# A transformer block with a mixture of experts: when the hidden rows are turned, and which engine loads the slot records of extra tokens

## The reference

```
x <- x + W_out [ gnorm(stick-breaking attention(h)) ++ gnorm(sliding-window GQA(h)) ] + b_out,  h = RMSNorm(x)
logits = RMSNorm(x) @ w_router + b_router          # 32 experts
top 4 of 32 per token, softmax over the four = gates
per chosen expert e, per token row:
    gu  = row @ w_gate_up[e] + b_gate_up[e]         # 1024 -> 2048
    act = (clip(up, -7, 7) + 1) * g * sigmoid(1.702 g),   g = min(gate, 7)
    y   = act @ w_down[e] + b_down[e]               # 1024 -> 1024
x <- x + sum of gate * y over the four;  output RMSNorm_final(x)
```

## Time and profile before

| | |
|---|---|
| median of 3 runs | 2253.32 us (2247.72 to 2255.8) |
| profiled execution | 2252.55 us, span 2250.4 us |
| granted TensorE clock, mean | 0.95 |
| busy: TensorE / VectorE / ScalarE / POOL | 94% / 68% / 65% / 14% |
| chain that ended last | TensorE 71%, VectorE 12%, issue 9%, ScalarE 4% |
| expert loop | item 0 starts at 768.49 us, the last item ends at about 2209 us |

### The profile page before, as it was taken

One profiled execution on the slowest core, in us unless ns is written; L12 is line 12 of the kernel. 1 busy time (PEld: TensorE's weight loads), 2 busy tenths in 40 slices (PEclk: granted clock), 3 DMA queues, 4 the chain that ended last, 5 costly groups with the idle time before them and its releaser, 6 DMA issues.

```text
span 2250.4 us, 37586 instructions
## 1 busy us (share of the span) xinstructions
PE 2108.3 (94%) x11367; PEld 1606.5 (71%) x11368; DVE 1521.1 (68%) x1908; ACT 1468.0 (65%) x1944; POOL 323.4 (14%) x327
## 2 busy tenths in 40 slices
PE   5999999999988499999999999999999999999997
PEld 4777777777766377878777777777776777676683
DVE  4355455553545678888888777787786688675585
ACT  4456565653332378888788687787785687675583
POOL 1000000001123211202011121111111121010022
PEclk9899999958989599999999999999999999999996
DMA  6300000110113789999899898899897899797694
GB/s 193 60 24 19 19 20 19 50 73 29 58 39 116 266 268 381 370 381 372 292 342 334 289 342 291 298 377 296 290 376 244 282 338 318 279 313 242 221 318 176
DMA packets 250409, 507.19 MB, mean 225 GB/s; under 512 B 44454, under 2 KB 62676, under 8 KB 250228
## 3 DMA queue, kind: packets, MB, share of 16 engines
q1 hardware_dynamic: 234724, 462.98, 58.4%
q0 software_dynamic: 15632, 43.53, 7.5%
HBM read 470.25 MB, written 38.54 MB: 226 GB/s over the span
## 4 chain that ended last, share of the span: by engine, by line
PE 71%; DVE 12%; issue 9%; ACT 4%; DMA 2%; POOL 1%; SPq 0%; DVEq 0%; ACTq 0%; POOLq 0%
PE bank L1001 23%; PE bank L1023 12%; PE bank L773 8%; PE bank L1035 6%; DVE w_low L1799 6%; PE bank L871 4%; PE bank L1052 3%; PE bank L826 2%; PE bank L853 2%; PE bank L801 2%; PE bank L816 2%; PE bank L842 2%; PE bank L1117 1%; PE bank L991 1%; DVE act_low L1813 1%
## 5 line engine op out<-in xcount | busy, mean ns | idle before, releaser
L1799 DVE TENSOR_TENSOR w_low<-gu_w,w_high 128x1024 fp32r<-128x1024 f32 x528 | 620.0, 1223 | 242.2 <-ACT w_high L1357 234.0
L1357 ACT CAST w_high<-gu_w 128x1024 fp32r<-128x1024 f32 x528 | 534.9, 1050 | 163.4 <-PE bank L1001 86.7
L1001 PE MATMUL bank<-w_high,x_high 128*128 128x512 f32 x1056 | 416.1, 394 | 3.0 <-DVE w_low L1799 3.0
L1001 PE MATMUL bank<-w_high,x_low 128*128 128x512 f32 x1056 | 413.9, 392 | 0.0
L1001 PE MATMUL bank<-w_low,x_high 128*128 128x512 f32 x1056 | 413.3, 391 | 0.0
L1799 DVE TENSOR_TENSOR w_low<-dn_w,w_high 128x1024 fp32r<-128x1024 f32 x264 | 315.1, 1225 | 19.5 <-ACT w_high L1357 13.2
L1357 ACT CAST w_high<-dn_w 128x1024 fp32r<-128x1024 f32 x264 | 270.8, 1050 | 23.1 <-PE bank L1001 13.4
L1023 PE MATMUL bank<-w_high,act_high 128*128 128x512 f32 x528 | 212.6, 403 | 23.9 <-DVE act_low L1813 23.9
L1001 PEld LDWEIGHTS bank<-w_high,x_high 128*128 128x128 f32 x1056 | 199.0, 188 | 46.6 <-DVE w_low L1799 3.8
L1001 PEld LDWEIGHTS bank<-w_high,x_low 128*128 128x128 f32 x1056 | 198.8, 188 | 42.8
L1001 PEld LDWEIGHTS bank<-w_low,x_high 128*128 128x128 f32 x1056 | 199.1, 189 | 42.1
(11 more groups left out here) (223 smaller groups left out, 3136.7 us busy)
## 6 DMA issues: line engine op xcount, KB each, us to landing
gu_w<-in_w_gate_up SPq DMA_DIRECT2D x528, 512.0 KB, 11.3
dn_w<-in_w_down SPq DMA_DIRECT2D x132, 1024.0 KB, 18.4
w_st<-in_w_in SPq DMA_DIRECT2D x14, 512.0 KB, 4.8
xt<-in_x SPq DMA_DIRECT2D x8, 512.0 KB, 4.4
wo_sb<-in_w_out SPq DMA_DIRECT2D x2, 2048.0 KB, 9.7
x<-in_x SPq DMA_DIRECT2D x8, 512.0 KB, 4.2
residual_rows<-x SPq DMA_DIRECT2D x8, 512.0 KB, 2.7
h_rows<-h SPq DMA_DIRECT2D x8, 512.0 KB, 2.9
```

The costliest lines, as they stand in the source:

```text
L1001: mm = pe.matmul(bank[:, 2 * h + g, :], a[:, k, :], b, start=False, stop=last)
L1357: act.copy(w_high[:, u % RING, :], src).then_inc(high_ready, 1)
L1799: dve.tensor_tensor(w_low[:, u % RING, :], raw, w_high[:, u % RING, :], ALU.subtract).then_inc(split_ready, 1)
```

## The change

On TensorE the second half is turned after three down units instead of four. On ScalarE `silu` follows `room` directly in both halves, with the casts that stood between them behind; the cast of unit 23 goes behind `act_high`. VectorE's order follows: the product of each half stands directly behind the clamp, unit 23's split behind `act_low`.

The six loads of the extra rows' records leave SP's `load_slots`. ScalarE issues them (`over_slots`), in the branch of `extra_rows` in which the next item has extra tokens, ahead of the wait for `xo_psum`. They count on a semaphore of their own, `d_over_slot`, which the other branch raises by the same 96. For their addresses ScalarE loads the next item's expert and first slot into registers in every pass, waits for the item's own `d_over_slot` and steps `act_passed`. POOL's `scatter` and ScalarE's `gated_rows` wait for `d_over_slot` too.

```diff
-SLOT_LOADS = 16 * (2 + sum(PARTS))
+SLOT_LOADS, OVER_LOADS = 16 * 2, 16 * sum(PARTS)
...
                 words(0, 0, P, 0, 0)
                 words(0, 1, EXTRA, P, 0)
-                word = 2
-                for k, parts in enumerate(PARTS):
-                    m = P // parts
-                    for q in range(parts):
-                        words(m * q, 2 + k, m, P, word)
-                        word += 2
...
             def scatter(n, step):
                 n_tok = tokens_of(n)
                 pool.wait_ge(slots_ready, n + 1)
+                pool.wait_ge(d_over_slot, OVER_LOADS * n + OVER_LOADS)
...
-                down(i, range(4))
+                down(i, range(3))
                 turn_hidden(i, 1)
+                down(i, range(3, 4))
                 by_class(n_tok, lambda parts: turn_over(i, parts))
...
+            def over_slots(n, e, first):
+                word = 2
+                for k, parts in enumerate(PARTS):
+                    m = P // parts
+                    for q in range(parts):
+                        act.dma_start(slot_in[m * q:m * q + m, bass.ds(8 * n + (12 + 2 * k), 2)],
+                                      slots[e, bass.ds(first + P, m), word:word + 2]).then_inc(d_over_slot, 16)
+                        word += 2
+
-            def extra_rows(n, n_tok):
+            def extra_rows(n, n_tok, e, first):
                 with act.If(n_tok > P):
+                    over_slots(n, e, first)
                     act.wait_ge(xo_psum, n + 1)
                     act.copy(xo[:], ...).then_inc(xo_ready, 1)
                 with act.Else():
                     act.sem_inc(xo_ready, 1)
+                    act.sem_inc(d_over_slot, OVER_LOADS)
...
             def gated_rows(n, n_tok):
                 act.wait_ge(slots_ready, n + 1)
+                act.wait_ge(d_over_slot, OVER_LOADS * n + OVER_LOADS)
...
                 room(i, 0)
-                high_part(i, range(12, 13))
                 silu(i, 0)
-                high_part(i, range(13, 17))
+                high_part(i, range(12, 17))
                 act_high_part(i, 0)
                 high_part(i, range(17, 20))
                 room(i, 1)
+                silu(i, 1)
                 high_part(i, range(20, 21))
-                silu(i, 1)
                 over_silu(i, n_tok)
-                high_part(i, range(21, 24))
+                high_part(i, range(21, 23))
                 act_high_part(i, 1)
+                high_part(i, range(23, 24))
                 over_turned(i, n_tok)
                 x_high_part(i + 1)
-                extra_rows(i + 1, n_next)
+                e = act.value_load(item_tab[0:1, bass.ds(i + 1, 1)], min_val=0, max_val=NE - 1)
+                first = act.value_load(item_tab[0:1, bass.ds(i + (2 * MAX_ITEMS + 1), 1)], min_val=0, max_val=SLOTS - ITEM)
+                act.wait_ge(d_over_slot, OVER_LOADS * i + OVER_LOADS)
+                act.sem_inc(act_passed, 1)
+                extra_rows(i + 1, n_next, e, first)
...
                 clamp(0)
-                low_part(range(12, 13))
                 hidden_out(0)
-                low_part(range(13, 17))
+                low_part(range(12, 17))
...
                 clamp(1)
+                hidden_out(1)
                 low_part(range(20, 21))
-                hidden_out(1)
...
-                low_part(range(21, 24))
+                low_part(range(21, 23))
                 act_low_part(1)
+                low_part(range(23, 24))
                 x_low_part(i + 1)
```

More of the change, by code:

```diff
@@ L255, in program @@
         d_empty, d_record, d_pad = sem("d_empty"), sem("d_record"), sem("d_pad")
-        d_slot = sem("d_slot")
+        d_slot, d_over_slot = sem("d_slot"), sem("d_over_slot")
         d_scatter = sem("d_scatter")
@@ L1335, in x_high_part @@
                              ).then_inc(x_high_ready, 1)
-            def extra_rows(n, n_tok):
+            slots = slot_dram.rearrange("(e r) w -> e r w", e=NE)
+            def over_slots(n, e, first):
[7 more added lines that the diff above has]
+            def extra_rows(n, n_tok, e, first):
                 with act.If(n_tok > P):
+                    over_slots(n, e, first)
                     act.wait_ge(xo_psum, n + 1)
@@ L1428, in _ @@
             x_high_part(0)
-            extra_rows(0, tokens_of(0))
+            extra_rows(0, tokens_of(0), 0, 0)
             act.wait_ge(tables_ready, 2)
```

## The result

Before: 2251.72 us, median of 4 runs (2247.72 to 2255.8). After, on the same chip: 2292.42 us (2289.95 to 2294.38). The ratio is 1.018, 95% interval 1.0158 to 1.0202: the change makes the kernel 1.8% slower. The span of the profiled execution went from 2250.4 to 2290.1 us, +39.7.

The account below looks back on a forecast made before the run. TensorE was taken to bound the kernel, except VectorE at the edge between items. Terms -2.9 - 3.1 + 35.5 + 5.7 + 0.5 = +35.7 on the profiled 2252.55 gave 2288 us, range 2275 to 2303.

Parts of the forecast that it names:

- The order: TensorE's waits for act_low between items: turning the second half after three down units alone gains 18.6 us.
- Value loads: ScalarE between token casts and table load: two loads, wait and step add 1.45 us per item, uncovered.
- Six issues: ScalarE before extra items: six slot loads take 4.1 or 3.8 us, adding 35.5 us after plain items, 5.7 after extra ones.
- Rival D: TensorE behind the new stalls: the clock falls, 5 us lost behind each, +40, 2328 us; 13%.
- the base: The main forecast for the whole kernel, without clock fall: 2288 us, given 50%.
- SP's queue and the start: Six loads fewer on SP: nothing in the loop; at the start -3.2, then ScalarE's six +3.1 to 4.1, net +0.5.
- Rival C: SP's and ScalarE's queues hold each other up: six loads take 8 us where weights stream, 2319 us; 15%.
- B: ScalarE before extra items: six issues cost only 1.0 us while value loads stay dear, 2255 us; 12%.
- A: ScalarE's additions come to under 0.7 us, unit 0 isn't late and all waits go, 2231 us; 10%.

Follow-up runs that it names:

- the value loads alone: Kernel before with the new order plus ScalarE's two value loads, wait and semaphore step, all slot loads on SP: 2239.08 us, ratio 0.9945.
- the filler: Changed kernel with 16 useless matmuls ahead of unit 0 in extra-token items that follow a plain item (item 0 too): 2274.79 us, ratio 1.0108.
- the loads alone: Changed kernel with all edits of order undone, value loads and the six slot loads still on ScalarE: 2295.34 us, ratio 1.020.
- the run with two loads: Changed kernel with only the two 64-row loads issued by ScalarE, the four of 32 rows on SP: 2262.8 us, ratio 1.0047.

## Why the prediction was right

The time came out at 2292.4, 4 us above the forecast and well inside the range, and the mechanism is the one forecast: the wait removed is no help, because ScalarE's path to unit 0 ends last. That the number came so near is luck: two errors cancelled.

*The order.* Transposes and `act_low` moved as said (928.21 for the estimated 927.84, TensorE at 929.03 for 928.7). By itself the order brings 23 us, 18.6 and some more: the items before extra ones lost their 0.7 and the extra ones 0.6 where 0.39 was the visible wait.

*Value loads.* 1.50 us in plain items for the 1.45 of the prediction; the ten plain before plain -2.6 for -2.0. Before an extra item they cost less: the stretch from token casts to unit 0's cast, 4.18 in the kernel before (1077.01 to the 1081.19 of the earlier trace rows), is 5.13 with the value loads alone, so 0.95. The rest lies beside the transposes of the extra rows, for which the copy waits there, as ScalarE's rows of the kernel with the value loads alone show:

```profile
1076.09 1.07 ACT L1335 CAST x_high<-bank 128x512 fp32r<-128x512 f32 x2 [0.30 <-PE bank L969]
1078.06 0.59 ACT L1341 COPY xo<-bank 128x512 f32<-128x512 f32 x1 [0.90 <-PE bank L977]
1079.92 1.28 ACT L1358 ACT_TABLE_LOAD   x1 [1.27 <-issue]
1081.22 3.90 ACT L1358 CAST w_high<-gu_w 128x1024 fp32r<-128x1024 f32 x4
```

*Six issues.* The stretch is 9.00 in the changed kernel (1076.02 to 1085.02, the cast of unit 0), 3.87 more: SP's rows, with 4.1, were the right ones to take. Token casts 0.13 later, 0.95 + 3.87 on ScalarE, and 2.36 from cast to unit 0 where there were 3.62, slack included: +3.7 in this item, +3.5 on average, for +4.4 predicted. **This term was mis-sized by 7.5 us** over eight items, mostly because it added the value loads in full, with none of them covered. The Trainium skill, DMA: Bandwidth & Descriptors, section Issuing engines are not separate DMA queues, calls the time to initiate a DMA usually small relative to the DMA itself. The trace agrees, 0.6 us for a landing of 4.7; but six of them stand on the path that ends last.

*Rival D.* It was given 13% and 5 us behind each stall. It happened, behind 8 of 8, at 1.5 to 2.75 us: +17.3. **This is the step that failed**: the base took no clock fall, on the ground that idles up to 1.48 had left the clock at 1.00. The one longer idle that it had looked at, 3.18, was followed by 0.50, and stalls of over 4 us stood on that side; the chance was too low and the price too high. Without it the extra items come out as follows: the five before an extra one +2.3 (13.6 less 11.3) for +5.7, the nine before a plain one -5.0 (1.0 less 6.0) for -3.1.

*The sum.* Without the slow clock it is +22.4 (the span with the filler is +21.6, its own gains and losses elsewhere included); with it 39.7. +35.7 was near because 12.8 too much (7.5 before extra items, 3.4 and 1.9 behind them) stood against 17.3 too little.

*SP's queue and the start.* Rival C is out. Behind an extra item (11) SP issues nothing beside ScalarE's six loads; behind a plain one (13) it issues weight loads for nearly all of that time, and the six take the same time. ScalarE, then SP at the second place:

```profile
1257.43 3.29 ACTq L1340 DMA_DIRECT2D slot_in<-slot_rows  x6
...
1346.18 3.30 ACTq L1340 DMA_DIRECT2D slot_in<-slot_rows  x6
```
```profile
1345.09 3.85 SPq L507 DMA_DIRECT2D dn_w<-in_w_down  x3
```

Over all places the six take 3.29 us behind extra items and 3.30 to 3.45 behind plain ones; those of item 7 (3.44) are among the longest (ns minimum, median, maximum):

```profile
L1340 ACTq DMA_DIRECT2D slot_in<-slot_rows x6: 331/372/556, 1078.3 to 1081.2; - x6
...
DMA to landing us min/median/max: 4.6/4.7/5.4
```

The Trainium skill, Perfetto Trace Analysis, section DMA Instruction — HWDGE, has a DMA instruction's recorded time hold the wait for a lock on a generator that two sequencers share. If it acts here, it costs the six 0.16 us at most. At the start the gather's indices are copied 2.47 us behind the first slot load instead of 5.74, the -3.2 of the prediction, as these two rows against the earlier trace rows show:

```profile
748.46 0.96 SPq L500 DMA_DIRECT2D slot_in<-slot_rows  x2
```
```profile
750.93 0.18 POOL L656 COPY gather_idx<-slot_in 128x4 int32<-128x4 int32 x1 [3.31 <-DMA slot_in<-slot_rows]
```

From the first slot load to unit 0 it is 25.4 us for 25.9; the +1.1 of the table is 1.7 of work ahead of this stretch, which varies from run to run, less this gain.

*Issues cheap, all hidden (B, A).* Out: the six cost 3.87, not 1.0, and beyond the slack of this path everything came through.

**Left open.** Why 2 of 8 stalls of 1.8 to 1.9 us left the clock alone, and one of 8 each of 2.6 and of 3.2 to 3.6; why the six issues ahead of item 0, whose addresses are constants, last 0.43 to 0.61 us each. The length of a slow stretch isn't open: it goes with where in the stall the clock falls, as the last section shows.

## What to carry to other kernels

A removed wait is worth what the next path behind it allows: before moving work, measure the slack of every path that ends at the same instruction (here 1.7 us on ScalarE), and put nothing on the one that has least. A DMA issue costs its engine's sequencer about 0.6 us; issue from a queue that nobody awaits, even if it is busier. And price a stall of TensorE by its length plus what the clock takes behind it: here a stall of 4.0 us cost another 2.2 behind it, and matmuls of no use in the gap won that back.

## What the runs showed of the hardware

The clock falls behind gaps that seem small in an engine that is otherwise full. Behind the 28 idles of up to 1.48 us in the loop of the kernel before it never fell; 1.8 to 1.9: 6 of 8; 2.6: 7 of 8; 3.2 to 3.6 (the loads alone): 7 of 8; 4.0: 8 of 8; gap filled: none.

It falls between 2.0 us ahead of the first matmul behind the gap and 1.3 behind it (1089.1 against 1087.79 in the run with two loads). The earliest is in item 14 of the changed kernel, unit 0 and the window from the fall on:

```profile
1355.14 0.79 PE L996 MATMUL bank<-w_high,x_high 128*128 128x512 f32 x1 [3.99 <-DVE w_low L1813]
```
```profile
1353.20:1360.00 6.80, 4.86 (x11) 3.80 (x12) 5.99 (x6) 6.36 (x7) 1.50 (x2) 0.50 1.03 406
```

Where it falls decides how long it stays low. In the four kernels with loads on ScalarE and no filler, all 7 stretches of 6.8 us begin 0.8 to 2.0 ahead of that matmul, and all 21 of 3.4 begin at most 0.4 ahead of it, or behind it. A longer stall leaves more room for an early fall: of the 4.0 us ones six of eight were long, of those of 2.6 and less none. The cost shows as longer matmuls in an item without a wait: in the changed kernel against the filled one 1.5 and 1.8 us for a low stretch of 3.4, 1.9 to 2.75 for one of 6.8.

A load of 32 rows issued by ScalarE on its own queue lands in 4.7 us (median); the same loads on SP's queue land in 12.6, behind the weights. Nothing needed them earlier here, so that gain was worth nothing.
